# Adding sums bank by bank, turning by quarters, another entry of a feed-forward stage, a maximum in one instruction, a store in two parts

## The reference

```python
h = x
for layer in range(2):
    if layer == 1:
        shared_kv = shared_moba_kv(h, ...)            # from the same h as the next line
    h = h + 0.5 * swiglu(rms_norm_2(h, ffn1_norm_g[layer]), ...)   # stages 0 and 2
    hn = rms_norm_2(h, mix_norm_g[layer])
    ...                                               # convolution (layer 0) or attention (layer 1)
    h = h + concatenate([primary, mem_out]) @ w_o[layer]
    h = h + 0.5 * swiglu(rms_norm_2(h, ffn2_norm_g[layer]), ...)   # stages 1 and 3

def swiglu(x, w_gate, w_up, w_down):
    return (silu(x @ w_gate) * (x @ w_up)) @ w_down
```

## Time and profile before

| | |
|---|---|
| runs | 1804.49, 1804.61, 1805.25 us |
| the profiled execution | 1805.91 us, of which the span from first to last instruction is 1803.9 us |
| busy | TensorE 92% of the span, weight loads 74%, VectorE 53%, ScalarE 38% |
| chain that ended last | TensorE 71%, DMA 20% (expert weights), VectorE 5%, ScalarE 3% |
| granted TensorE clock, mean | 0.974 of full |

### The profile page before, as it was taken

One profiled execution on the slowest core, in us unless ns is written; L12 is line 12 of the kernel. 1 busy time (PEld: TensorE's weight loads), 2 busy tenths in 40 slices (PEclk: granted clock), 3 DMA queues, 4 the chain that ended last, 5 costly groups with the idle time before them and its releaser, 6 DMA issues.

```text
span 1803.9 us, 30839 instructions
## 1 busy us (share of the span) xinstructions
PE 1666.8 (92%) x12691; PEld 1342.0 (74%) x12706; DVE 964.5 (53%) x1626; ACT 693.6 (38%) x1035; POOL 49.3 (3%) x53
## 2 busy tenths in 40 slices
PE   6998999787878787899999989999999999999998
PEld 6987866564555554688879768888788888678887
DVE  4776451111111110666668767676767677557666
ACT  5444451011001100544454155445644454454443
POOL 2000000000000000010000400000000000000000
PEclk9999999999999898999999989999999999899999
DMA  9634369999999999665555024655455553135560
GB/s 301 207 135 168 117 233 389 427 430 428 428 429 430 428 427 415 216 208 172 178 163 187 0 94 163 209 176 173 145 205 194 169 173 117 48 103 187 176 209 24
DMA packets 167981, 409.53 MB, mean 227 GB/s; under 512 B 5351, under 2 KB 137598, under 8 KB 155628
## 3 DMA queue, kind: packets, MB, share of 16 engines
q1 hardware_dynamic: 166048, 404.54, 59.6%
q0 software_dynamic: 1632, 4.01, 0.8%
q10 hardware_dynamic: 236, 0.06, 0.0%
HBM read 407.54 MB, written 1.05 MB: 226 GB/s over the span
## 4 chain that ended last, share of the span: by engine, by line
PE 71%; DMA 20%; DVE 5%; ACT 3%; issue 1%; SPq 0%; ACTq 0%; DVEq 0%
PE bank L1083 18%; DMA odd_expert<-in_w_up_dram 15%; PE bank L567 10%; PE bank L569 10%; PE bank L568 10%; PE bank L1085 9%; DMA odd_expert<-in_w_gate_dram 4%; PE bank L894 3%; PE bank L1064 2%; PE bank L682 2%; PE bank L708 1%; DVE wlo L1745 1%; PE bank L919 1%; DVE x L1783 1%; ACT whi L1285 1%
## 5 line engine op out<-in xcount | busy, mean ns | idle before, releaser
L1083 PE MATMUL bank<-x,whi 128*128 128x512 f32 x1408 | 502.5, 400 | 7.8 <-DVE wlo L1745 6.6
L1085 PE MATMUL bank<-x,wlo 128*128 128x256 f32 x1408 | 396.3, 281 | 0.0
L1083 PEld LDWEIGHTS bank<-x,whi 128*128 128x128 f32 x1408 | 265.7, 189 | 76.0 <-DVE wlo L1745 7.2
L2256 DVE TENSOR_TENSOR wlo<-raw,whi 128x2048 fp32r<-128x2048 f32 x120 | 273.9, 2310 | 34.6 <-ACT whi L1603 29.1
L1085 PEld LDWEIGHTS bank<-x,wlo 128*128 128x128 f32 x1408 | 267.1, 190 | 1.5
L1603 ACT ACTIVATE whi<-raw 128x2048 fp32r<-128x2048 f32 x120 | 225.3, 1912 | 60.6 <-PE bank L569 60.6
L1745 DVE TENSOR_TENSOR wlo<-raw,whi 128x2048 fp32r<-128x2048 f32 x67 | 152.9, 2288 | 63.4 <-ACT whi L1285 62.5
L1285 ACT ACTIVATE whi<-raw 128x2048 fp32r<-128x2048 f32 x67 | 127.1, 1908 | 44.9 <-PE bank L569 38.7
L567 PE MATMUL bank<-whi,hh_hi 128*128 128x512 f32 x352 | 138.7, 394 | 0.0
L569 PE MATMUL bank<-wlo,hh_hi 128*128 128x512 f32 x352 | 137.7, 391 | 0.0
L568 PE MATMUL bank<-whi,hh_lo 128*128 128x512 f32 x352 | 137.2, 390 | 0.0
(11 more groups left out here) (333 smaller groups left out, 2337.0 us busy)
## 6 DMA issues: line engine op xcount, KB each, us to landing
raw<-in_ffn_w_gate_dram SPq DMA_DIRECT2D x44, 1024.0 KB, 5.2
raw<-in_ffn_w_up_dram SPq DMA_DIRECT2D x44, 1024.0 KB, 6.6
raw<-in_ffn_w_down_dram SPq DMA_DIRECT2D x44, 1024.0 KB, 6.0
raw<-in_w_gate_dram SPq DMA_DIRECT2D x16, 2048.0 KB, 20.9
raw<-in_w_up_dram SPq DMA_DIRECT2D x16, 2048.0 KB, 24.2
raw<-in_w_down_dram SPq DMA_DIRECT2D x16, 2048.0 KB, 24.3
odd_expert<-in_w_gate_dram SPq DMA_DIRECT2D x16, 2048.0 KB, 26.4
odd_expert<-in_w_up_dram SPq DMA_DIRECT2D x16, 2048.0 KB, 26.4
```

What stands on the lines that cost most here:

```text
L1083: pe.matmul(bank[:, :], hi[:, k, :], x_both[x][:, k, :, :].rearrange("p b n -> p (b n)"), start=k == 0, stop=False, skip_group_check=True)
L1085: mm = pe.matmul(bank[:, 0:TOK], lo[:, k, :], xhi[x][:, k, :], start=False, stop=k == KT - 1, skip_group_check=True)
L2256: dve.tensor_tensor(wlo[:, c0_ % SPLIT, :], raw[:, c0_ % RAW, :], whi[:, c0_ % SPLIT, :].bitcast(F32), ALU.subtract).then_inc(lo_ready, 1)
```

## The change

- `add_to_h` and the end of `swiglu` on VectorE wait for each of the four banks by itself. TensorE increments `outer_half` and `ffn_half` after each of the first three banks of the last product, where it did so once, after the second. Each add into `h` in `swiglu` increments `h_tile`, where there were two increments for four adds.
- `turn` has a way by quarters, used for the four turns that read `h` directly (in stages 1, 2 and 3, and before the projections of layer 1): the first two fills of token tile 0 after bank 0's add, of tile 1 after bank 2's, then the other two fills.
- Third stage (q = 2): the second turn is issued behind the first half of the gate product (`beside_gate`), and VectorE splits the stage's second chunk (up) ahead of the row scale instead of behind it.
- The 12 causal heads use `negated_max`: for each token tile one instruction that adds mask and scores, scales by -0.125, writes that out and reduces it to the minimum, which is the negated maximum. The exponential is taken with scale -1. The four heads of the first block keep `causal_max`.
- The store is issued per token tile, the first when its two banks are added.

```diff
@@ build
+        def banks_added(c0):
+            return tuple((evac_v, evac_count[c0 + i][1]) for i in range(4))
+        def updated(q):
+            return tuple((h_tile, 4 * q + (2 + i)) for i in range(4))
@@ SP
-            sp.wait_ge(h_ready, 9)
-            sp.dma_start(out[0].rearrange("(t p) d -> p t d", p=P), h[:, :, :]).then_inc(out_done, 16)
-            sp.wait_ge(out_done, 16)
+            for tt in range(TT):
+                sp.wait_ge(h_tile, 15 + 2 * tt)
+                sp.dma_start(out[0][tt * P:tt * P + P, :], h[:, tt, :]).then_inc(out_done, 16)
+            sp.wait_ge(out_done, 32)
@@ TensorE, turn
+                if quarters:
+                    for half in range(2):
+                        for tt in range(TT):
+                            pe.wait_ge(*half_ready[2 * tt + half])
+                            for i in range(2 * half, 2 * half + 2):
+                                mm = tiles(i, tt)
+                                if tt == TT - 1:
+                                    mm.then_inc(tr_done, 1)
+                    n["turn"] += fills
+                    return
@@ TensorE, linear_outer (and the same in swiglu with ffn_half)
-                        if i == 3 and j == 1 and tt == 0:
-                            mm.then_inc(outer_half, 1)
+                            if i == 3 and j == 1 and 2 * tt + half < 3:
+                                mm.then_inc(outer_half, 1)
@@ TensorE, swiglu, pair
                     gate_or_up(gate, 0, ps[4], True).then_inc(gate0_done, 1)
+                    if first and beside_gate is not None:
+                        beside_gate()
@@ TensorE, order of the stages
-            turn(h, added(c0 + 7))
+            turn(h, banks_added(c0 + 7))
...
-            turn(h, ((h_tile, 3), (h_ready, 6)))
-            turn(h, ((h_tile, 3), (h_ready, 6)))
-            swiglu(2, 0, late_clear=True)
+            turn(h, updated(1))
+            swiglu(2, 0, late_clear=True, beside_gate=lambda: turn(h, updated(1)))
             keep_busy(2, ps[7])
-            turn(h, ((h_tile, 4), (h_ready, 7)))
+            turn(h, updated(2))
...
-            turn(h, added(c0 + 10))
+            turn(h, banks_added(c0 + 10))
@@ ScalarE, attend
-                            exps(CAUSAL_W, prob_slot(n["unit"]), 1.0, False)
+                            exps(CAUSAL_W, prob_slot(n["unit"]), -1.0, False)
@@ VectorE, add_to_h
-                    if i == 0:
-                        dve.wait_ge(outer_half, n["outer"])
-                    if i == 2:
+                    if i < 3:
+                        dve.wait_ge(outer_half, 3 * n["outer"] + (i - 2))
+                    else:
                         used(c0 + 3)
@@ VectorE
+            def negated_max(bias, mult):
+                u = n["unit"]
+                slot, nm = prob_slot(u), nmax[:, stat_cols(u)]
+                dve.wait_ge(s_full, u + 1)
+                if slot_free(u):
+                    dve.wait_ge(t_done, slot_free(u))
+                for tt, cols_ in enumerate((slice(0, P), slice(P, CAUSAL_W))):
+                    ins_ = dve.tensor_tensor_reduce(slot[:, cols_], ps[4 + u % 2][:, cols_], bias[:, cols_], -mult, 3.0e38,
+                                                    ALU.add, ALU.min, nm[:, tt:tt + 1])
+                ins_.then_inc(nm_ready, 1)
+                n["unit"] += 1
@@ VectorE, end of swiglu
                 for tt in range(TT):
-                    if tt == 0:
-                        dve.wait_ge(ffn_half, q + 1)
-                    else:
-                        dve.wait_ge(chunk_used, s + 3 * PAIRS)
                     for half in range(2):
+                        if 2 * tt + half < 3:
+                            dve.wait_ge(ffn_half, 3 * q + (2 * tt + half + 1))
+                        else:
+                            dve.wait_ge(chunk_used, s + 3 * PAIRS)
                         dst = h[:, tt, half * 512:half * 512 + 512]
-                        ins_ = dve.scalar_tensor_tensor(...)
-                    ins_.then_inc(h_tile if tt == 0 else h_ready, 1)
-                dve.wait_ge(h_ready, (4, 6, 7, 9)[q])
+                        dve.scalar_tensor_tensor(...).then_inc(h_tile, 1)
+                dve.wait_ge(h_tile, 4 * q + 5)
@@ VectorE, before stage 2
             split_turned(0, G_FFN1 + 8)
+            split_to(ffn_starts[2] + 2)
             row_scale()
             diagonal_scales()
```

More of the change, by code:

```diff
@@ L573, in turn @@
                 first = n["turn"]
-                half_ready = gained if isinstance(gained[0], tuple) else ((gained[0], max(gained[1] - 1, 1)), gained)
+                quarters = isinstance(gained[0], tuple)
+                half_ready = gained if quarters else ((gained[0], max(gained[1] - 1, 1)), gained)
                 def tiles(i, tt):
@@ L581, in tiles @@
                     return mm
-                pe.wait_ge(*half_ready[0])
+                if not quarters:
+                    pe.wait_ge(*half_ready[0])
                 ahead = min(fills, 4 if first // 4 in WIDE_TURNS + (KV_TURN,) else 2)
@@ L1124, in pair @@
                                                    lo[:, j, half * 512:half * 512 + 512], False, last and j == 1)
-                            if last and j == 1 and tt == 0:
-                                mm.then_inc(ffn_half, 1)
+                                if last and j == 1 and 2 * tt + half < 3:
+                                    mm.then_inc(ffn_half, 1)
                     mm.then_inc(chunk_used, 1)
@@ L1623, in _ @@
             swiglu(0, mem2_keys)
-            row_stats(h, ((h_tile, 2), (h_ready, 4)))
+            row_stats(h, (updated(0)[1], updated(0)[3]))
             split_turned(0, G_MIX2)
@@ L2261, in swiglu @@
                 for tt in range(TT):
-                    if tt == 0:
-                        dve.wait_ge(ffn_half, q + 1)
-                    else:
-                        dve.wait_ge(chunk_used, s + 3 * PAIRS)
                     for half in range(2):
+                        if 2 * tt + half < 3:
+                            dve.wait_ge(ffn_half, 3 * q + (2 * tt + half + 1))
+                        else:
+                            dve.wait_ge(chunk_used, s + 3 * PAIRS)
                         dst = h[:, tt, half * 512:half * 512 + 512]
-                        ins_ = dve.scalar_tensor_tensor(dst, ps[2 * tt + half][:, :],
-                                                        0.5 if q < 1 else half_rstd[:, tt:tt + 1], dst, ALU.mult, ALU.add)
-                    ins_.then_inc(h_tile if tt == 0 else h_ready, 1)
-                dve.wait_ge(h_ready, (4, 6, 7, 9)[q])
+                        dve.scalar_tensor_tensor(dst, ps[2 * tt + half][:, :], 0.5 if q < 1 else half_rstd[:, tt:tt + 1], dst,
+                                                 ALU.mult, ALU.add).then_inc(h_tile, 1)
+                dve.wait_ge(h_tile, 4 * q + 5)
             normed_rows(h)
```

14 lines of the change are left out of this document (6 added, 8 removed).

## The result

| | before | after |
|---|---|---|
| runs, median | 1804.93 us (4 runs, 1804.49 to 1807.23) | 1795.84 us (4 runs, 1793.9 to 1796.25) |
| ratio | | 0.9945, interval 0.9928 to 0.9962 |
| span of the profiled execution | 1803.9 | 1793.8 |

By the medians the change gains 9.1 us. The forecast was 4.3 (1800.3 us), and its range ended at 1796.3: the direction was right, the size was not.

The account below looks back on a forecast made before the run. TensorE's own work was taken as seven tenths of the span, so gains lay in gaps between stages. 0.6 + 0.7 + 1.75 - 0.9 + 0.9 + 1.3 = 4.35 us off 1804.6 gave 1800.3 us, range 1796.3 to 1802.6.

Parts of the forecast that it names:

- the head loop: Layer 1's causal heads: half-clock stretches counted as unchanged, the maximum gains 0.9 us, quarters before the projections 0.63.
- the fall expected in stage 2: Third stage: a new 2.1 us stand before the down product halves the clock, making the stage's net -0.9 us.
- the 0.6 behind the memory attention: At 244.4, behind the memory attention's output: one add less after the last product, 0.6 us gained.
- Adds bank by bank: Adds follow the products where VectorE is free: 0.6 us behind the memory attention, 0.7 at the kernel's end.
- the expert loads, which set the time, are issued from that work: From 304 on: why the 0.6 us gained behind the memory attention should last.
- Quarters: Gaps before stage 1, stage 3 and the projections: ScalarE's split starts earlier by 0.57, 0.55 and 0.63, together 1.75 us.
- The third stage's order: Up half starts 1.6 us earlier, but the row scale starts later: 0.35 gained, -0.9 us with a new clock fall.
- Transposes: Third stage's 16 deferred transposes: expected not to lower the clock; rival that they count as idle, 1802.0 us, chance 0.05.
- The maximum: Causal heads: instruction pair takes 0.8 us instead of 1.11, 0.3 gained at three TensorE waits, 0.9 us; bounds +1.5 and -0.9.
- the low clock goes away in more places: Rival: half-clock stretches vanish in the head loop or third stage, 1794 to 1799, say 1797.5 us; chance 0.20.
- The prediction's own sign of being wrong: Forecast wrong if the clock's falls change in number, the new instruction exceeds 0.6 us, or the second store lands equally late.
- The store: Kernel's end: the second store has half the data to move after the last add, 1.3 us less.

Follow-up runs that it names:

- entry_undone: Changed kernel with the third feed-forward stage entered as before (both turns in front, up chunk split behind the row scale): 1795.58 us.
- adds_alone: Kernel before with only the adds bank by bank and the turns by quarters: 1801.17 us.
- before_filled: Kernel before with eight products of zeros put in front of TensorE's two waits at step 6 of the head loop: 1800.65 us.
- max_undone: Changed kernel with the old three-instruction maximum in the 12 causal heads: 1803.08 us.
- after_again: Changed kernel run again without any edit: 1795.68 us.
- before_shift8: Kernel before with eight more products of zeros ahead of layer 1's projections, to start the head loop later: 1805.12 us.
- after_shift12: Changed kernel with twelve more products of zeros ahead of layer 1's projections, to start the head loop later: 1796.74 us.
- more_filled: Changed kernel with the old order of stage 2 and products of zeros in TensorE's long waits, including those at 159 and 1516: 1787.82 us.

## Why the prediction was wrong, point by point

The step that failed is the head loop. The sum put its clock at nothing, leaving the 13.7 us at half clock where they were, and the maximum at 0.9 us; with 0.63 for the quarters this part was to gain 1.53 us and gained 7.30. In the place of that nothing the runs show 4 to 5 us of clock, and in the place of the 0.9 some 1.7 (1.5 to 2.6). The other terms together gave 3.7 us where the forecast had 2.8: the fall expected in stage 2 did not come (1.3 more), and the 0.6 behind the memory attention was lost.

- **Adds bank by bank.** At the end 0.68, forecast 0.7. Behind the memory attention the gain arrived where I said: the first expert's refill came 100.10 us behind the adds at 172 instead of 100.89. But from it to the adds at 727 the changed kernel took 454.77 instead of 454.08, in the 13 profiles with the new adds 454.3 to 455.6 (mean 454.8), in the five with the old ones 453.8 to 454.4 (mean 454.2). The step "the expert loads, which set the time, are issued from that work" failed. The refills of the first 56 us kept their distances to 0.01 us in before and after; behind that they wander by up to 1.7 us either way, and the stretches at half clock lie at other places there. What eats the 0.7 was not found; it stays open.
- **Quarters.** 0.63 and 0.65 twice, forecast 0.57, 0.55 and 0.63. ScalarE's square was late next as I wrote.
- **The third stage's order.** Taken with the fall of before as the reference, the 0.35 without a new fall came out as 0.37. What failed in it is the clock: I expected the new stand to be followed by a fall because those of 2.49, 1.94 and 1.35 had been. The stand was 1.6 us, not 2.1 (TensorE had waited 0.26 for the row before it), and no fall came; in entry_undone none came behind 2.07 us. The deeper error is that the fall was not part of the old order: with the quarters it was not there (entry_undone, adds_alone). Against the old order without a fall the new one is a loss of 1.8 us. The hidden tile was ready 21.3 us behind the first add, 21.4 in the forecast, so the new order was reckoned rightly. But it was set against a down product of before (1284.01) that the fall itself had made late, and so 0.35 looked like a gain of the order.
- **Transposes.** Sixteen of them stood behind the gate's half at 1269.67, and the clock stayed at 1.00 behind them. By the rule of the Trainium skill (TensorE: Matmul & The Clock Gate, Part 4: PE-mode transpose) they would not count as busy. This trace does not bear it out, nor does entry_undone, where neither 28 in a row (1262.33 to 1265.37) nor the stand of 2.07 us that came 2.8 us after them was followed by a fall.
- **The maximum.** The pair was 0.55 us, a little under the 0.6 of my nearest rows, not 0.8; I had stepped up from the nearest row by caution without a row behind it. The Trainium skill (Vector Engine (DVE) Microarchitecture Reference, Points that are easy to get wrong) has the throughput halved for two SBUF sources in a type other than bf16. Here one source is a bank, and at 0.42 us for 256 columns, the plain add's time, nothing is halved. The three places were right (the second stands at 1538.9, not 1536.8): 0.56, not 0.3, at each, 1.73 us instead of 0.9. Other comparisons give 1.5 to 2.6.
- **The clock in the head loop.** This is the term that decided. I gave "the low clock goes away in more places" 0.20 and 1797.5, with "they stay above 1.3 us" against it. In the changed kernel the stands at step 6 were 0.47 and 0.91 us (1.02 and 0.92 before), and the stretch of 13.7 us was gone, one of 3.4 had grown to 6.8. With 17.1 us at half clock before and 6.8 after, the clock can give half of 10.3, 5.1 us, at most; the products of zeros in before_filled gave 5.0 to 5.6. Of the 7.3 us of this part, 0.65 to 0.72 are quarters, 1.5 to 2.6 the maximum (1.7 by its waits), and the rest, 4 to 5, the clock. The prediction's own sign of being wrong, that the falls change in number, came: those at 1274 and 1554 were gone. The rival was right in kind and its bounds (1794 to 1799) held the result; the range on record cut it at 1796.3.
- **The store.** 1.24 and 1.26, forecast 1.3.

Sizes once more, by the forecast's terms: 0.6 became 0.1, 0.7 became 0.68, 1.75 became 1.93 (quarters of stage 1, projections, stage 3), -0.9 became 0.37, 0.9 became some 1.7, 1.3 became 1.24, and up to 5 of clock came on top; the start and the stretch from 727 to 1072, where little was changed, took 0.9 of it back in this pair of profiled executions.

## What to carry to other kernels

Before a gap's order is costed, the half-clock stretches behind it have to be taken out of the reference: a change may look even because it trades a loss of work for a fall that did not happen. Here the new order of stage 2 lost 1.8 us and looked like a gain of 0.4. A term that hangs on the clock is a matter of likelihood: cost it both ways, give the better way a real chance, and don't let the range cut it. The cheap remedy is on TensorE itself: products of zeros in front of its long waits, with the old order of stage 2, gave 8 us here (1.8 of it the order), nearly as much as the whole change.

## What the runs showed of the hardware

- For one kernel, max_undone, the runs spread over 9 us (1796.9 to 1806.1), against 1.2 us for after_again, and the shorter ones have the higher mean granted clock (0.978 to 0.981, against 0.973 to 0.976). A single execution of such a kernel settles little.
- The length of a stand did not by itself tell whether the clock fell behind it: 2.49 us in front of stage 2's up half was followed by a fall in 4 of 4 kernels, 2.07 us at the same place in none of 2, 0.47 and 0.91 us at step 6 by a stretch in 3 of 8.
- With the head loop some 1.1 to 2.2 us later and unchanged inside, one execution had 3.4 us where before had 13.7 (before_shift8) and one had 3.4 where there was none (after_shift12). That the shift did this is not shown.
- The part ahead of the adds at 172 took from 170.4 to 173.6 us in these profiles, though only more_filled adds work there. The clock goes with it: the 12 profiles with 3.4 us at half clock both at 83 and at 161 have 172.3 to 173.6, the six others 170.4 to 171.9. That is more than most terms of the sum, so single parts are compared from adds to adds, not by the end.
- An instruction on VectorE that combines two operands, one from a bank, writes them and reduces them on the way took no longer than the plain add (0.29 and 0.42 us), and 0.09 more to read the result.
